# First unit of the last expert's weights: nine transfers by rows of partitions in place of one

## What is computed

```python
def clamped_swiglu(h):
    glu, lin = jnp.split(h, 2, axis=-1)
    glu = jnp.minimum(glu, 7.0)
    lin = jnp.clip(lin, -7.0, 7.0)
    return glu * jax.nn.sigmoid(1.702 * glu) * (lin + 1.0)

# for each expert e, tokens x_e routed to it (top 4 of 32 by softmax of the router)
y_e = clamped_swiglu(x_e @ w1[e] + b1[e]) @ w2[e] + b2[e]     # w1: 1024 x 2048, w2: 1024 x 1024
out = layer_norm(alpha * h + sum_e weight_e * y_e) * ln2_w + ln2_b
```

## Time and profile before

| | |
|---|---|
| median of 3 runs | 1315.06 us (1313.43 to 1315.21) |
| profiled execution, its own time | 1314.36 us |
| its span, first to last instruction | 1312.6 us |
| TensorE matmul busy | 1255.9 us, 96% of the span |
| moved by DMA | 458.99 MB, 350 GB/s over the span |
| granted TensorE clock, mean | 0.994 |

### The profile page before, as it was taken

The page is one execution under the profiler, slowest core; times in us unless marked ns, Lnnn a source line. Parts: engine busy times, 40 slices in busy tenths (PEclk is TensorE's granted clock), DMA queues, the critical chain, the costliest instruction groups (busy, mean ns, idle before and its releaser), DMA issues.

```text
span 1312.6 us, 15073 instructions
## 1 busy us (share of the span) xinstructions
PE 1255.9 (96%) x6092; PEld 640.3 (49%) x6092; DVE 455.3 (35%) x916; ACT 216.7 (17%) x424; POOL 4.0 (0%) x20
## 2 busy tenths in 40 slices
PE   9999999999999999999999999989999898999996
PEld 8788888998753333333333333333333333333332
DVE  4679965366347122121221212122121212222123
ACT  1432224221031101101011010101101010110101
POOL 0000000000000000000000000000000000000000
PEclk9999999999998999999999999999999999999999
DMA  9433344226778999999999999999999999999994
GB/s 367 163 145 136 112 145 160 103 98 233 284 326 344 408 432 431 431 433 432 432 429 431 432 431 431 431 430 431 431 431 431 432 430 431 431 431 431 425 429 191
DMA packets 28124, 458.99 MB, mean 350 GB/s; under 512 B 4352, under 2 KB 4736, under 8 KB 8992
## 3 DMA queue, kind: packets, MB, share of 16 engines
q1 hardware_dynamic: 24928, 454.04, 82.5%
q10 hardware_dynamic: 3136, 4.03, 0.9%
HBM read 457.02 MB, written 1.05 MB: 349 GB/s over the span
## 4 chain that ended last, share of the span: by engine, by line
PE 60%; DMA 25%; DVE 11%; ACT 2%; issue 1%; DVEq 0%; SPq 0%; ACTq 0%
DMA store<-in_moe_w 24%; PE banks L1156 15%; PE banks L1188 13%; PE banks L761 11%; PE banks L775 4%; PE banks L1162 4%; PE banks L1041 2%; PE banks L1091 2%; DVE store L1786 2%; PE banks L1210 1%; PE banks L1175 1%; DVE store L1783 1%; DVE store L1785 1%; DVE store L1780 1%; ACT store L687 1%
## 5 line engine op out<-in xcount | busy, mean ns | idle before, releaser
L1156 PE MATMUL banks<-store 128*64 128x512 f32 x1536 | 342.7, 595 | 26.4 <-DMA store<-in_moe_w 23.8
L1156 PEld LDWEIGHTS banks<-store 128*64 128x64 f32 x1536 | 111.4, 137 | 241.2 <-issue 209.1
L1188 PE MATMUL banks<-store 128*64 128x512 f32 x1024 | 227.8, 597 | 0.0
L761 PE MATMUL banks<-store 128*128 128x256 f32 x896 | 196.4, 380 | 0.0
L761 PEld LDWEIGHTS banks<-store 128*128 128x128 f32 x896 | 169.5, 190 | 25.7 <-issue 3.0
L1780 DVE TENSOR_SCALAR store<-banks 128x512 f32<-128x512 f32 x32 | 22.1, 691 | 444.2 <-PE banks L1162 444.2
L1188 PEld LDWEIGHTS banks<-store 128*64 128x64 f32 x1024 | 71.0, 137 | 155.4 <-issue 130.3
L1162 PE MATMUL banks<-store 128*64 128x512 f32 x512 | 116.9, 598 | 1.2 <-DMA store<-in_moe_w 1.2
L687 ACT ACTIVATE store<-store 128x512 f32<-128x512 f32 x32 | 20.2, 630 | 479.9 <-DVE store L1780 479.9
L1794 DVE COPY store<-banks 64x512 f32<-64x512 f32 x32 | 22.2, 694 | 221.0 <-PE banks L1188 221.0
L1091 PEld LDWEIGHTS banks<-store 128*128 128x128 f32 x480 | 57.0, 191 | 24.3 <-issue 23.5
(11 more groups left out here) (359 smaller groups left out, 827.1 us busy)
## 6 DMA issues: line engine op xcount, KB each, us to landing
store<-in_moe_w SPq DMA_DIRECT2D x81, 4096.0 KB, 38.0
store<-in_moe_w SPq DMA_DIRECT2D x30, 2048.0 KB, 14.7
store<-in_w_in SPq DMA_DIRECT2D x30, 1024.0 KB, 4.8
store<-in_w_branch SPq DMA_DIRECT2D x8, 1024.0 KB, 4.8
store<-in_w_out SPq DMA_DIRECT2D x4, 1024.0 KB, 6.7
store<-in_xT SPq DMA_DIRECT2D x2, 512.0 KB, 5.6
store<-in_w_in SPq DMA_DIRECT2D x2, 512.0 KB, 7.2
store<-in_s_w_glu SPq DMA_DIRECT2D x1, 1024.0 KB, 5.0
```

The lines of the kernel that those rows point to most:

```text
L761: last = mm(b[:, j * SEQ:(j + 1) * SEQ], w[:, k, j * P:j * P + P], xT[:, k, :], start=k == 0, stop=k == KD - 1)
L1156: last = mm(bank[i][64 * ct:64 * ct + 64, :], xg[:, 2 * c + kk, col:col + CAP], w[:, kk, i * FF + ct * 512:i * FF + ct * 512 + 512], start ...
L1188: last = mm(bank[4][64 * dh:64 * dh + 64, :], actT[:, j, 64 * fh:64 * fh + 64], w[:, j, 512 * dh:512 * dh + 512], start=(fh, j) == (0, 0), ...
```

## The change

The first unit of expert 31 (c = 0) is issued as nine transfers: eight of 8 partitions each, which cover partitions 0 to 63, and then one with partitions 64 to 127. The other five units stay one transfer each. TensorE's wait for unit 0 counts 9 x 16 in place of 16. The same bytes go from the same rows to the same places.

```diff
         LAST = (NE - 1) * NU
+        PARTS = [[slice(8 * i, 8 * i + 8) for i in range(8)] + [slice(64, P)]] + [[slice(0, P)]] * (NU - 1)
         ln2_w, ln2_b = unit_at(LAST - 4)[:, 0:D], unit_at(LAST - 4)[:, D:2 * D]
...
             for c in range(NU):
                 sp.wait_ge(S["expert_chunk_used"], LAST + c - 2 * NDBL + 1)
-                sp.dma_start(unit_at(LAST + c), unit_source(NE - 1, c)).then_inc(double_landed[c], 16)
+                for rows in PARTS[c]:
+                    sp.dma_start(unit_at(LAST + c)[rows, :], unit_source(NE - 1, c)[rows, :]).then_inc(double_landed[c], 16)
...
-                pe.wait_ge(double_landed[c], (NPAIR + 1) * 16 if c < NU // 2 else NPAIR * 16)
+                pe.wait_ge(double_landed[c], (NPAIR if c < NU // 2 else NPAIR - 1) * 16 + 16 * len(PARTS[c]))
```

## The result

| | before | after |
|---|---|---|
| median of 4 runs, us | 1315.13 (1313.43 to 1315.31) | 1332.84 (1332.13 to 1333.32) |
| profiled execution, us | 1314.36 | 1332.13 |
| its span, us | 1312.6 | 1330.4 |
| bytes moved, MB | 458.99 | 458.99 |

The ratio is 1.0139, with a 95% interval of 1.0126 to 1.0151: the change costs 17.7 us, three times what was forecast, and the time lies above the range (1313.5 to 1329.0). The direction was right, the size was not.

What follows compares the result with a forecast made beforehand. Weights landing at 430 GB/s were taken to bound the kernel, with 1.17 us waited for. The profiled 1314.36 plus 6.0 for unit 3's later landing gave 1320.4, as a median 1321.0; range 1313.5 to 1329.0.

Steps and rivals of the forecast that it cites:

- I take the twelve to fall to the early half: Unit 0 of expert 31: twelve rows go to the engine half finishing 6.2 us earlier, four to the other; chance 0.85.
- Rival D: Unit 0's twelve rows fall to the late half of engines: median 1317.5, or 1327.3 with contention; chance 0.08.
- The price of a narrow row: Unit 0's 8-partition transfers: a row costs 2.5 times a wide one, 12.2 us for eight, 1258.2 to 1270.4.
- The late half has four rows fewer ... if nothing else slows it: Later-finishing engines get four rows fewer of unit 0: 2.4 us earlier, also for everything behind; unit 3 at 1281.4.
- The 64-partition transfer at 2x, 4.9 us: Unit 0's partitions 64 to 127: four rows at twice the wide price, 4.9 us, early half done at 1275.3.
- The end: Expert 31: TensorE waits 3.4 us for unit 0; unit 3 lands at 1289.9, +6.0 us; no wait behind it.
- Issues: SyncE's eight extra issues take 2.7 us, nobody waits; a full queue at worst cuts the gain to some 0.4.
- The clock: TensorE's clock may fall to 1.2 GHz at the wait before unit 0: 0 to 3.5 us, slow side only.
- A: Narrow rows of unit 0 cost what wide ones do: 1313.2, median 1313.9; chance 0.22.
- B: Engines meeting at one partition group fall into file, 6.7 us instead of 12.2: +0.5, median 1315.6; chance 0.15.
- E: Unit 0's nine transfers stay spread evenly, eight rows for each engine: 1315 to 1321; chance 0.03.
- C: Narrow rows of unit 0 cost four times wide ones, 19.5 us: +13.3, median 1328.4; chance 0.17.

Runs made afterwards that it cites:

- e10: Changed kernel with the eight 8-partition transfers four partitions apart and partitions 64 to 127 of unit 0 not loaded: 1313.85 us, ratio 0.9998.
- e1: Changed kernel with each 8-partition transfer taking every fourth partition of 32, 64-partition transfer kept: 1325.86 us, ratio 1.0083.
- e4: Kernel before, with unit 0 of expert 31 as eight transfers of all 128 partitions, 512 columns each: 1315.33 us, ratio 1.001.
- e2: Changed kernel, narrow transfers still writing neighbouring partitions but reading source rows four apart: 1334.15 us, ratio 1.0152.
- e3: Changed kernel, narrow transfers writing partitions four apart but reading neighbouring source rows: 1328.05 us, ratio 1.0106.
- e9: Changed kernel with the eight neighbour transfers alone; partitions 64 to 127 of unit 0 not loaded: 1326.54 us, ratio 1.0091.
- e5: Kernel before, with unit 0 of expert 31 as two transfers, partitions 0 to 63 and 64 to 127: 1327.48 us, ratio 1.0085.
- e6: Kernel before, with unit 0 of expert 31 as two transfers, even and odd partitions: 1314.53 us, ratio 1.0002.
- e11: Changed kernel with each 8-partition transfer taking every second partition of 16, 64-partition transfer kept: 1331.59 us, ratio 1.0129.
- e8: Kernel before, with unit 0 of expert 31 as eight transfers of 16 neighbouring partitions: 1329.65 us, ratio 1.0101.
- e12: Kernel before, with unit 3 of expert 31 in two column halves, each with its own semaphore and wait: 1313.59 us, ratio 0.9996.

## Why the prediction failed, step by step

**What bounds the kernel: right.** The stream of weights sets the pace up to unit 3, and unit 3's start moved by the whole loss.

**How many engines serve a narrow transfer: right.** The semaphore records show eight completions by engines for each, and sixteen for the 64-partition one. The Trainium skill (DMA: Bandwidth & Descriptors, "Why a DMA increments its semaphore by 16 and not by 1") says that a transfer uses the largest number of engines up to 16 that divides its rows; the records agree, with 8 for 8 partitions.

**"I take the twelve to fall to the early half": this step failed in part.** They fall to six engines of the early half and two of the late one (e10). The forecast had the early half land unit 3 last; in the change the last two are those two late engines, 2.7 and 5.2 us behind the other fourteen. Rival D had this case, for all eight. Four more wide rows cost each of the two 2.4 us even without any contention; the forecast had that in D alone.

**"The price of a narrow row", 2.5x, 12.2 us: about right.** On the six early engines the narrow stretch was forecast as 1258.2 to 1270.4; by unit 0's semaphore it was over near 1271.

**"The late half has four rows fewer ... if nothing else slows it": this is the step that failed most.** The forecast gave each half of the engines its own clock: contention was to cost only those that write to the crowded partitions, and the late half was to lose just its 2.4 us again. The runs show the whole stream slowed. In the window 1268 to 1274 the sixteen engines together moved 158 GB/s at a share of 0.96; eight engines at full rate alone would be 215. So the others must have been held back too. Every row of 16 KB that began between 1262 and 1274 took 1.06 to 2.08 us by the packet records, instead of 0.61. The landings say the same: for expert 30's unit 5, whole, equal and queued ahead, each of the late eight engines needed 11.2 to 12.0 us instead of 4.9, and it landed at 1273.8 instead of 1264.3. The half that lands last was thus late by up to 9.5 us before it had moved a byte of unit 0, and the lead of 6.2 us of the early half bought nothing.

**The 64-partition transfer at 2x, 4.9 us: too small.** e1 has it without crowded narrow rows. By the forecast's own numbers unit 3 would land there at 1258.2 + 4.9 + 4.9 + 14.6 = 1282.6, before the 1283.87 of the kernel before, so e1 would have cost nothing; it cost 11.7 us. Of that the twelve rows of the two late engines can explain 2.4. The forecast named a likely cause, that other engines write to the same partitions, and priced it for four rows of eight engines instead of for the whole stream.

**"The end": right in form.** No new wait behind unit 3, and its own wait of 1.24 us stayed.

**Issues: right.** Fourteen issues cost nobody anything, and neither did a full queue (e4).

**The clock: within its bounds.** 0 to 3.5 us were forecast. TensorE's clock fell twice here, and it cost nothing at the end; below.

**The rivals.** A (no extra price) and B (the engines fall into file) are refuted by the first window at 229 GB/s. E, an even spread, is refuted by the eight completions and by a time far outside 1315 to 1321. D is right for two of the eight engines and wrong for six: the rate fell before 1262, and the late half reaches unit 0 only at 1264.4. C, four to one all the way, gave 1328.4, nearest and still 4.4 us short, for the reason of the failed step: it too charged only eight engines. My range ended just above C; what it lacked was a case in which contention spreads to engines that write elsewhere.

**The cause, as far as it is shown.** Engines that write to the same few neighbouring partitions at one time are slow, and take the other engines with them. Shown: the destination decides (e2 against e3), neighbours against four apart (e9 against e10), lower and upper half against even and odd (e5 against e6). Not shown, but in line with all of them: in a whole-unit transfer each engine has partitions of its own. The narrow neighbours put eight engines on the same eight partitions, and a transfer of 64 neighbouring partitions sends half of the engines to partitions that the other half is writing. Four neighbours behave as one place: one row in each group of four is free (e10), two are not (e11).

The same account as a rule on ways into SBUF: the Trainium skill (SBUF — State Buffer, "Door 1: The DMA port swizzle") says that a transfer is as fast as the number of sixteen ports that its partitions reach, where four neighbours share a port and the partition 32 further has the same one. By it e6 reaches all sixteen and is free, e5 reaches eight for each half, and e8 four, so that unit 0 would take four times 4.88 us, 14.6 more as an estimate. e6 (no cost), e5 (194 to 238 GB/s) and e8 (14.9 us) agree. But by it e5 would cost only another 4.88 us, and it measured 12.7; e11, with twice the ports of the change, should be well below it, and was 0.8 us below. The measurement decides: the rule tells which of these cuts are slow, and not what they cost beside a full stream.

**Open.** Why engines that write elsewhere are held back; whether the order of the source rows costs anything (e2 and e3, 2.2 to 2.3 us above their counterparts); whether e8 costs less than the change (14.9 and 17.7 us, with intervals that overlap), as its even rows would have it. Which rows each engine has in a wide or a 64-partition transfer is inferred, not read.

## What to carry to other kernels

Where a stream of wide loads runs at full rate, cut a load along its columns (e4, e12: no cost that these runs can tell) or into every second partition (e6), and not into blocks of neighbouring partitions: two plain halves of one 2 MB unit cost 12.7 us here, the eight narrow pieces 17.7. Judge DMA by GB/s, not by its busy share, which stood near 1.00 while the rate was 158. Read the semaphore of a landing engine by engine: it shows which engines come last. And price contention on the whole stream with the transfers already queued ahead, not on the engines that cause it; before that, ask what is to be gained (1.17 us here).

## What the hardware showed that was not expected

The rate of all sixteen engines fell together, to 158 to 279 GB/s for 30 us, because of one unit of 2.1 MB. The eight engines of a narrow transfer are not one of the two halves that finish together: six are early, two late. One issue of SyncE stood 12.9 us in e4, with no cost.

In this stretch TensorE's granted clock fell to 0.50, 1.2 GHz, twice, each time while TensorE stood in a wait (those of 5.51 and 8.03 us); this is the first fall:

```profile
1270.80:1277.60 6.80, 3.76 (x10) 1.25 (x12) 0.00 (x0) 0.00 (x0) 0.00 (x0) 0.50 0.95 202
```

Each of the two groups of 16 matmuls took 5.5 us for 3.6. This cost nothing at the end, since TensorE waited for unit 3 anyway: a faster group would have waited longer.
